# A two-block transformer layer on one core: the first block's steps in another order, and the memory's keys projected while experts are chosen

## The chip, the core and the metric

The kernel runs on one core of one Trainium2 chip. TensorE multiplies matrices and transposes, VectorE (DVE) and ScalarE (ACT) do the elementwise work, GpSimd (POOL) clears two tiles, and SyncE (SP) issues nearly all DMAs. Everything is in fp32. The metric is the device time of one execution in microseconds; lower is better.

## The reference

Two transformer blocks run one after the other on 256 tokens of width 1024. The first block has two mixers, a merge of both, and a layer of 64 experts. The second has three attention branches; the keys and values of one (cross attention) come from a second input, the memory, and from nothing that the first block computes.

```python
def first_block(x, ...):
        h = rmsnorm(x, attn_norm_w[l])
        z = h @ w_in[l]
        hq, hf, hi, hg, cq, ckv, kr, gate_a, gate_b = jnp.split(z, split_idx, axis=-1)
        o_a = hgrn2_mixer(hq, hf, hi, hg, lb_all[l], hg_out_norm_w[l]).astype(x.dtype)
        o_b = mla_mixer(cq, ckv, kr, positions, mla_q_norm_w[l], mla_w_uq[l], mla_kv_norm_w[l], mla_w_ukv[l])
        y = jax.nn.sigmoid(gate_a) * (o_a @ w_branch_hgrn[l]) + jax.nn.sigmoid(gate_b) * (o_b @ w_branch_mla[l])
        x = x + y @ w_out[l]
        h = rmsnorm(x, ffn_norm_w[l])
        x = x + hierarchical_moe(h, router_group_w[l], ...)   # top group, then its top 2 of 8 experts
    return rmsnorm(x, final_norm_w)

def hybrid_layer(x, mem, ...):
    h = rmsnorm_2(x, g_in)
    z = h @ w_in
    ...
    kv = rmsnorm_2(mem, g_mem) @ w_mem_kv
    xk = kv[..., :X_W].reshape(B, M, X_HEADS, X_HEAD_DIM)
    xv = kv[..., X_W:].reshape(B, M, X_HEADS, X_HEAD_DIM)
    yc = cross_attention(heads(xq, X_HEADS, X_HEAD_DIM), xk, xv).reshape(B, S, X_W)
    ...
    return x + u @ w_out
```

## The kernel before

**The plan.** `plan()` writes a list of steps, and every engine walks through the same list in the same order, taking from each step the part that is its own. So the list fixes the order on each engine, and semaphores tie the engines together. The steps that matter here:

- `proj` of a name is a projection of all 256 tokens by one unit of weights (mostly 1024 x 512): 32 matmul instructions of 256 columns (features in rows, L803) or 16 of 512 (tokens in rows). The hardware profiler records two passes for each fp32 matmul, so its counts are twice these; transposes are recorded once. Projections take turns on the PSUM tiles psP0 and psP1; all other steps use psA and psB.
- `hf`, `hq`, `hv`, `hg` belong to the first mixer (forget gate, queries, values, output gate). `level` 0 to 8 build its causal attention in nine steps: TensorE multiplies (L948), VectorE copies under a mask (L1511) and makes the operands of the next level by four products (L1298). A projection stands between any two levels.
- `cl` and `ch` give the latents of the second mixer, `cnorm` normalises them: squares and roots on ScalarE (L1214 to L1220), scaling on VectorE (L1537, L1538), 10 transposes on TensorE, a scaled copy on VectorE. `uq` projects queries from them, `kn` keys, `vm` values; `hg_out`, `hg_outT` finish the first mixer and transpose it; `qkpT` transposes the rotary parts.
- `scores` (TensorE, psA, L1029 and L1030), `soft` (VectorE scale and maximum, ScalarE exponentials), `normal` (VectorE division), `probsT` (TensorE transposes into psB, ScalarE copies out) and `pv` (TensorE into psB, VectorE copies out) do attention in three chunks, 0 to 2.
- `ga`, `gb` are gates; `wa` and `wb` project the mixers' outputs, `wo` the merged one, `rt` is the router. `norm mem` normalises the memory and transposes it (16 transposes). `rank` chooses the experts: a chain of small VectorE steps, five small matmuls (L1071 to L1075), again VectorE.
- `moe` is the expert loop. All weights of 64 experts go through four buffers of 4 MB, 96 chunks in all. TensorE first gathers tokens (32 passes, L467), then each chunk takes 32 or so passes (L481, L492). `xk`, `xv` project keys and values of the memory, at the start of the second block, while ScalarE and VectorE do its first norm (`stats`).

**Where weights lie.** Units go through `ring`, four slots of 2 MB. SyncE loads unit n when unit n-4 has been multiplied. The first four expert chunks are not allowed in before a projection each has finished (`before_chunk`: wb1, wo0, wo1, wo1), since they take the place of ring slots and of tiles in the `arena`. Chunk c from 4 on waits for `used`, a count that TensorE raises behind each chunk it has finished, to reach c-3.

**Where steps wait for each other.** The wait of a `proj` step on TensorE covers its weights, its PSUM tile (emptied by ScalarE or VectorE) and its inputs. wb0 waits for the last `pv`, wo0 for the evacuation of wb1. The MoE part of TensorE waits for `rt`, for the selection matrix and for the normalised tokens.

Of the kernel before, what the change touches and what calls it, by code (L numbers as in the profile page):

```python
# [29 lines left out]
S = 256  # L30
NT = S // P
D = 1024
KC = D // P
# [76 lines left out]
def units_2():  # L110
    kv = [("xk", "w_mem_kv_2", 0, 512, 8), ("xv", "w_mem_kv_2", 512, 512, 8)]
    u = [("iq", 4096), ("ikw", 4608), ("dq", 2048), ("dv", 3072), ("dk", 2560), ("mv", 1024), ("mq", 0),
         ("dg", 3584), ("mk", 512), ("mg", 1536)]
    u = kv + [(n, "w_in_2", c, 72 if n == "ikw" else 512, 8) for n, c in u]
    u += [("xq", "w_in_2", 4680, 512, 8), ("xg", "w_in_2", 5192, 512, 8)]
    u += [(f"gl{i}", "w_in_2", 5704 + 512 * i, 512, 8) for i in range(6)]
    u += [("um", "w_up_moba_2", 0, 1024, 4), ("ud", "w_up_dsa_2", 0, 1024, 4), ("ux", "w_up_cross_2", 0, 1024, 4)]
    u += [(f"w2{i}", "w_out_2", 512 * i, 512, 8) for i in range(2)]
    return u


UNITS_1, UNITS_2 = units_1(), units_2()


# [17 lines left out]
def plan():  # L142

    p = []
# [19 lines left out]
    proj("hf0", "hf1", "hq0", "hq1")  # L164
    p.append(("level", 0, "AB"))
    fill = [["hv0"], ["hv1"], ["cl"], ["ch"], ["hg0", "hg1"], ["ga0"], ["ga1"], ["gb0"]]
    for n in range(1, len(LEVELS) + 2):
        proj(*fill[n - 1])
        p.append(("level", n, "AB" if n <= len(LEVELS) else "A"))
    p.append(("cnorm", 0, "AB"))  # L170
    p.append(("hg_out", 0, "AB"))
    proj("gb1")
    proj("uq0n", "uq0p", "uq1n", "uq1p")
    p.append(("hg_outT", 0, "AB"))
    p.append(("qkpT", 0, "AB"))
    proj("kn0", "kn1")
    soft(0)
    proj("vm0", "vm1")
    turn(0, 1, "wa0")
    turn(1, 2, "wa1")  # L180
    p.append(("normal", 2, ""))
    p.append(("norm", "mem", "AB"))
    p.extend([("probsT", 2, "B"), ("pv", 2, "B")])
    proj("wb0", "wb1")
# [5 lines left out]
    proj("rt")  # L190
    p.append(("rank", 0, "A"))
    p.append(("moe", 0, ""))

    p.append(("stats", "mid", ""))
    proj("xk", "xv")
# [71 lines left out]
def build(nc, ins, out):  # L267
    with ExitStack() as ctx:
# [62 lines left out]
        memT = area(1, KC, S)  # L331
        mem = area(13, NT, D)
# [8 lines left out]
        xqT, xkT, xv = area(8, 4, S), area(8, 4, S, off=1024), area(9, NT, 512)  # L341
        ropeA, ropeB = area(9, NT, 512, off=1024), area(13, NT, 512)
        relu_s = area(13, 2, 512, off=1024)
# [5 lines left out]
        wrow, wrow_f = cT[:, 0:4, :].rearrange("p a b -> p (a b)"), area(13, D, off=1024)  # L349
# [36 lines left out]
        rt_in = sem("rt_in")  # L386
# [50 lines left out]
        def unit_ap(name):  # L437
            slot, _, _, (_, _, _, cols, kc) = unit_at[name]
            return ring[:, slot, 0:kc * cols].rearrange("p (k n) -> p k n", k=kc)

        def wait_unit(e, name):
            e.wait_ge(unit_at[name][1], unit_at[name][2])
# [16 lines left out]
        def moe_tensor(pe):  # L459
# [53 lines left out]
            pe.wait_ge(no_rows, 1)  # L513
            with pe.Fori(0, rounds) as r:
# [195 lines left out]
        def _(sp):  # L710
# [77 lines left out]
        def _(pe):  # L788
# [6 lines left out]

            def proj(key, name, lhs_of, rhs_of, kc, outs):

                may_fill(pe, key)
                r = region_of(key)
                for o in range(len(outs(ps[r]))):  # L800
                    dst = outs(ps[r])[o]
                    for k in range(kc):
                        mm = pe.matmul(dst, lhs_of(o, k), rhs_of(o, k), start=(k == 0), stop=(k == kc - 1))  # L803
                mm.then_inc(full[r], 1)
# [19 lines left out]
            for name, arg, _ in PLAN:  # L824
                key = (name, arg)
# [255 lines left out]
        def _(act):  # L1081
# [31 lines left out]
            for name, arg, _ in PLAN:  # L1113
                key = (name, arg)
                if name == "norm":
# [6 lines left out]
                    elif arg == "mem":  # L1122
                        act.wait_ge(mem_in, 16)
                        wait_full(act, ("scores", 2))
                        square_sums(lambda t: mem[:, t, :], lambda t: memT[:, :, :].rearrange("p k s -> p (k s)")[:, t * D:(t + 1) * D], 2, 16, D)
# [162 lines left out]
        def _(dve):  # L1288
# [68 lines left out]
            for name, arg, _ in PLAN:  # L1357
# [41 lines left out]
                elif name == "norm" and arg == "mem":  # L1399
# [3 lines left out]
                    i.then_inc(normed, 1)  # L1403
                    into_T(key, memT, V_MEM)
# [285 lines left out]
def laid_out(inputs):  # L1690

    given = {name: np.ascontiguousarray(inputs[name]) for name in _AS_THEY_ARE}
    for name, tensor, c0, cols, kc in UNITS_1 + UNITS_2:
# [47 lines left out]
```

## Time and profile before

| what | us |
|---|---|
| median of 3 runs | 1761.36 (1760.98 to 1761.41) |
| the profiled execution's own time | 1762.46 |
| its span, first to last instruction | 1760.6 |
| TensorE busy | 1384.9 |
| VectorE busy | 329.5 |
| ScalarE busy | 209.0 |
| mean granted TensorE clock | 0.893 of full speed |
| DMA | 504.43 MB, mean 287 GB/s |

The first block's mixers fill the first 430 us or so, the expert loop the next 920, the second block the last 410. The span is the figure to set a sum of the trace against; the run around it adds 1.9 us. In the tables below, idle time before an instruction stands in brackets with the engine that ended it.

### The profile page before, as it was taken

The numbers are of one execution on the slowest core, as the hardware profiler recorded it, in microseconds if no ns is written. First come the engines' busy times: TensorE is split into PE (matmuls) and PEld (weight loads), VectorE is DVE, ScalarE is ACT, GpSimd is POOL, SyncE is SP. The second block draws the span as 40 slices with busy tenths as digits, with TensorE's granted clock in tenths as the row PEclk, the third lists the DMA queues.
The fourth block names the chain that finished last, engine by engine and source line by source line (L and its number), as shares of the span: only waits on it lengthen the run. The fifth ranks groups of instructions, "written<-read, shape, count | busy, mean of one in ns | idle before, by whom it ended". The sixth has DMA issues, their size and how long they took to land.

```text
span 1760.6 us, 16409 instructions
## 1 busy us (share of the span) xinstructions
PE 1384.9 (79%) x7184; PEld 778.7 (44%) x7184; DVE 329.5 (19%) x585; ACT 209.0 (12%) x366; POOL 1.4 (0%) x6
## 2 busy tenths in 40 slices
PE   6999989888866676656666666666667999999996
PEld 5756886775322122212221222122214546788882
DVE  2233432312211001101010101010101221252221
ACT  1000032202000000000000000000001001143300
POOL 0000000000000000000000000000000000000000
PEclk9999998988987788878887888888878999999998
DMA  7324133317999999999999999999997433332310
GB/s 285 114 103 172 67 117 146 102 51 330 394 429 433 433 431 429 433 434 432 429 430 435 433 429 430 435 433 430 430 435 337 171 134 137 132 144 108 142 50 24
DMA packets 24550, 504.43 MB, mean 287 GB/s; under 512 B 4672, under 2 KB 4928, under 8 KB 6336
## 3 DMA queue, kind: packets, MB, share of 16 engines
q1 hardware_dynamic: 24080, 503.69, 68.6%
q8 instruction: 30, 0.49, 0.1%
q10 hardware_dynamic: 432, 0.17, 0.0%
q14 instruction: 8, 0.07, 0.0%
HBM read 502.81 MB, written 1.05 MB: 286 GB/s over the span
## 4 chain that ended last, share of the span: by engine, by line
PE 51%; DMA 44%; DVE 3%; ACT 1%; issue 1%; SPq 0%; DVEq 0%; ACTq 0%
DMA arena<-in_experts 44%; PE psP L803 35%; PE psP L481 5%; PE psP L492 3%; DVE arena L1298 2%; PE psB L1064 1%; PE psB L793 1%; PE psA L948 1%; PE psB L948 1%; PE psA L1030 1%; PE psA L1029 1%; PE psA L793 0%; PE psA L502 0%; PE psP L848 0%; PE psP L842 0%
## 5 line engine op out<-in xcount | busy, mean ns | idle before, releaser
L803 PE MATMUL psP<-arena,ring 128*128 128x256 f32 x1664 | 369.3, 384 | 2.2 <-DVE arena L1298 1.4
L803 PEld LDWEIGHTS psP<-arena,ring 128*128 128x128 f32 x1664 | 319.1, 193 | 48.1 <-issue 4.2
L481 PE MATMUL psP<-ring,arena 128*32 128x512 f32 x1024 | 162.1, 792 | 103.9 <-DMA ring<-in_experts 103.9
L803 PE MATMUL psP<-ring,arena 128*128 128x512 f32 (+2 forms) x576 | 233.1, 564 | 7.3 <-DVE arena L1298 7.3
L481 PE MATMUL psP<-arena 128*32 128x512 f32 x1024 | 158.1, 774 | 99.8 <-DMA arena<-in_experts 99.8
L1298 DVE TENSOR_TENSOR X<-X,psA 128x512 f32<-128x512 f32 x68 | 46.8, 688 | 682.1 <-PE psA L502 682.1
L803 PEld LDWEIGHTS psP<-ring,arena 128*128 128x128 f32 x576 | 105.7, 191 | 126.1 <-issue 126.0
L481 PEld LDWEIGHTS psP<-ring,arena 128*32 128x32 f32 x1024 | 41.0, 139 | 223.2 <-issue 176.5
L481 PEld LDWEIGHTS psP<-arena 128*32 128x32 f32 x1024 | 37.3, 136 | 217.9 <-DMA arena<-in_experts 126.5
L492 PE MATMUL psP<-arena 128*32 128x512 f32 x512 | 76.8, 754 | 53.6 <-DMA arena<-in_experts 49.8
L492 PE MATMUL psP<-ring,arena 128*32 128x512 f32 x512 | 73.4, 725 | 48.0 <-DMA ring<-in_experts 44.5
L467 PEld LDWEIGHTS psA<-arena 128*128 128x128 f32 x544 | 64.0, 197 | 15.1 <-issue 15.1
L502 PE MATMUL psA<-arena 128*128 128x512 f32 x136 | 67.4, 618 | 2.0 <-ACT arena L578 1.2
L467 PE MATMUL psA<-arena 128*128 128x128 f32 x544 | 67.2, 283 | 1.2 <-DVE small L627 1.2
L492 PEld LDWEIGHTS psP<-arena 128*32 128x32 f32 x512 | 18.1, 134 | 106.4 <-DMA arena<-in_experts 61.8
L1298 DVE TENSOR_TENSOR arena<-arena 128x1024 f32<-128x1024 f32 (+6 forms) x90 | 63.1, 729 | 1.2
L492 PEld LDWEIGHTS psP<-ring,arena 128*32 128x32 f32 x512 | 17.9, 129 | 97.9 <-issue 46.7
L1108 ACT ACTIVATE arena<-psP 128x1024 f32<-128x1024 f32 (+1 forms) x26 | 26.1, 1002 | 286.7 <-PE psP L803 286.7
L571 ACT ACT_TABLE_LOAD x16 | 20.5, 1283 | 276.6 <-PE psP L481 276.6
L573 ACT ACTIVATE arena<-psB 128x256 f32<-128x256 f32 x16 | 6.1, 383 | 333.3 <-PE psB L542 333.3
L578 ACT ACTIVATE arena<-psP 128x1024 f32<-128x1024 f32 x16 | 16.4, 1023 | 244.2 <-PE psP L492 244.2
L502 PEld LDWEIGHTS psA<-arena 128*128 128x128 f32 x136 | 23.0, 189 | 48.4 <-issue 44.6
(223 smaller groups left out, 748.3 us busy)
## 6 DMA issues: line engine op xcount, KB each, us to landing
arena<-in_experts SPq DMA_DIRECT2D x48, 4096.0 KB, 33.3
ring<-in_experts SPq DMA_DIRECT2D x48, 4096.0 KB, 33.3
ring<-in_u_gl SPq DMA_DIRECT2D x6, 2048.0 KB, 7.7
ring<-in_u_hf SPq DMA_DIRECT2D x2, 2048.0 KB, 11.9
ring<-in_u_hq SPq DMA_DIRECT2D x2, 2048.0 KB, 22.0
ring<-in_u_hv SPq DMA_DIRECT2D x2, 2048.0 KB, 7.7
ring<-in_u_hg SPq DMA_DIRECT2D x2, 2048.0 KB, 7.4
ring<-in_u_ga SPq DMA_DIRECT2D x2, 2048.0 KB, 7.5
```

Of the source, the lines that this page charges most:

```text
L467: mm = pe.matmul(zA[:, k * P:(k + 1) * P], xnf[:, t, k * P:(k + 1) * P], selA[:, t].rearrange("p j c -> p (j c)"), start=(t == 0), stop=(t ...
L481: mm = pe.matmul(z[j * CAP:(j + 1) * CAP, :], x[:, 4 * half + k, j * CAP:(j + 1) * CAP], held[c % 4][:, j, k * 512:(k + 1) * 512], start=( ...
L492: mm = pe.matmul(zY[j * CAP:(j + 1) * CAP, cols * 512:(cols + 1) * 512], hidT[:, 2 * half + f, j * CAP:(j + 1) * CAP], held[c % 4][:, j, f ...
L502: pe.matmul(zA[:, c:c + 512], selTs[:, t * P:(t + 1) * P], ysb[:, half * 512:(half + 1) * 512], start=True, stop=True).then_inc(scattered, 1)
L571: act.activation(gs, ps["P0"][:, 0:512], ACT.Silu).then_inc(gate_read, 1)
L793: mm = pe.transpose(ps[region][:, i * P:(i + 1) * P], src_of(i), ident)
L803: mm = pe.matmul(dst, lhs_of(o, k), rhs_of(o, k), start=(k == 0), stop=(k == kc - 1))
L948: mm = pe.matmul(ps[r][:, h * P:(h + 1) * P], k[:, h, t * P:(t + 1) * P], q[:, h, t * P:(t + 1) * P], start=True, stop=True)
L1029: pe.matmul(dst, qn[:, h, tt], kn[:, h, 0:nk], start=True, stop=False)
L1030: mm = pe.matmul(dst, qpeT[lo:lo + 64, h // 2, tt], kpeT[lo:lo + 64, 0:nk], start=False, stop=True)
L1108: act.activation(dst, view(ps[r]), func, **kw).then_inc(empty[r], 1)
L1298: return dve.tensor_tensor(o, a, b, op)
```

## The change

Five edits to the plan, and what they need:

1. `hv0` is projected ahead of level 0, and the other fillers between levels move up by one; `hg0` and `hg1` no longer stand together.
2. `cnorm` stands between level 5 and level 6, inside the projection `ga0`: 16 of its 32 matmuls, the latents' transposes, the other 16. A new step `head` runs a projection up to a given matmul and leaves it open in its PSUM tile. `gb1` now stands between level 8 and `hg_out`.
3. `kn0`, `kn1` stand ahead of `qkpT`, and `vm0` ahead of the first `scores`.
4. The last softmax: `scores` 2 and its softmax stay, but `probsT` 2 and `pv` 2 lie inside `wa1`, which is cut at 16 and 24 matmuls. The memory's statistics are a step `mnorm` behind `wa1`, and its 16 transposes stand behind `wb1`.
5. `xk` is projected around `rank`: 20 matmuls ahead of it, 12 behind. Its weights do not go through the ring any more. They have a place of their own (`wxk`, areas 10 and 11 of the arena), loaded behind the first expert chunk once `wb1` has been evacuated. `xkT`, `relu_s` and `wrow_f` change places in the arena. GpSimd waits for `xk` before it clears its tiles, which lie in area 11 and 13, and TensorE waits for the evacuation of `xk` before the loop.

```diff
 def units_2():
-    kv = [("xk", "w_mem_kv_2", 0, 512, 8), ("xv", "w_mem_kv_2", 512, 512, 8)]
+    kv = [("xv", "w_mem_kv_2", 512, 512, 8)]
...
-    proj("hf0", "hf1", "hq0", "hq1")
+    proj("hf0", "hf1", "hq0", "hq1", "hv0")
     p.append(("level", 0, "AB"))
-    fill = [["hv0"], ["hv1"], ["cl"], ["ch"], ["hg0", "hg1"], ["ga0"], ["ga1"], ["gb0"]]
+    fill = ["hv1", "cl", "ch", "hg0", "hg1", "ga0", "ga1", "gb0"]
     for n in range(1, len(LEVELS) + 2):
-        proj(*fill[n - 1])
+        if fill[n - 1] == "ga0":
+
+            p.append(("head", ("ga0", 16), ""))
+            p.append(("cnorm", 0, "AB"))
+        proj(fill[n - 1])
         p.append(("level", n, "AB" if n <= len(LEVELS) else "A"))
-    p.append(("cnorm", 0, "AB"))
+    proj("gb1")
     p.append(("hg_out", 0, "AB"))
-    proj("gb1")
     proj("uq0n", "uq0p", "uq1n", "uq1p")
     p.append(("hg_outT", 0, "AB"))
+    proj("kn0", "kn1")
     p.append(("qkpT", 0, "AB"))
-    proj("kn0", "kn1")
+    proj("vm0")
     soft(0)
-    proj("vm0", "vm1")
+    proj("vm1")
     turn(0, 1, "wa0")
-    turn(1, 2, "wa1")
+
+    p.append(("normal", 1, ""))
+    soft(2)
+    p.append(("probsT", 1, "B"))
+    p.append(("head", ("wa1", 16), ""))
+    p.append(("pv", 1, "B"))
     p.append(("normal", 2, ""))
+    p.append(("probsT", 2, "B"))
+    p.append(("head", ("wa1", 24), ""))
+    p.append(("pv", 2, "B"))
+    proj("wa1")
+    p.append(("mnorm", 0, ""))
+    proj("wb0", "wb1")
     p.append(("norm", "mem", "AB"))
-    p.extend([("probsT", 2, "B"), ("pv", 2, "B")])
-    proj("wb0", "wb1")
     proj("wo0")
...
     proj("rt")
+
+    p.append(("head", ("xk", 20), ""))
     p.append(("rank", 0, "A"))
+    proj("xk")
     p.append(("moe", 0, ""))
 
     p.append(("stats", "mid", ""))
-    proj("xk", "xv")
+    proj("xv")
...
+        wxk = area(10, KC, 512)
...
             pe.wait_ge(no_rows, 1)
+            wait_empty(pe, ("proj", "xk"))
...
                     sp.dma_start(held[c % 4].rearrange("p e n -> p (e n)"), src).then_inc(chunk_in[c % 4], 16)
+                    if peeled and c == 0:
+
+                        wait_empty(sp, ("proj", "wb1"))
+                        sp.dma_start(wxk, ins["u_xk"].rearrange("p (k n) -> p k n", k=KC)).then_inc(xk_in, 16)
...
             pool.wait_ge(rounds_ready, 1)
+            wait_full(pool, ("proj", "xk"))
             pool.memset(selTs, 0.0)
```

**The order on TensorE around the latents' norm.** Before, L948 and L954 are the levels, L803 projections (here `ga0`, `ga1`, `gb0`), L793 the latents' transposes and L973 `hg_out`:

```order
L948 MATMUL psA<-arena 128x128 x8
L948 MATMUL psB<-arena 128x128 x8
L803 MATMUL psP<-arena,ring 128x256 x32
L948 MATMUL psA<-arena 128x128 x8
L948 MATMUL psB<-arena 128x128 x8
L803 MATMUL psP<-arena,ring 128x256 x32
L954 MATMUL psA<-arena 128x128 x8
L793 MATMUL psA<-consts_sb,arena 128x128 x5
L793 MATMUL psB<-consts_sb,arena 128x128 x5
L973 MATMUL psA<-arena 128x128 x8
```

Of the change (L988, L994 the levels, L837 projections, L823 transposes):

```order
L988 MATMUL psA<-arena 128x128 x8
L988 MATMUL psB<-arena 128x128 x8
L837 MATMUL psP<-arena,ring 128x256 x16
L823 MATMUL psA<-consts_sb,arena 128x128 x5
L823 MATMUL psB<-consts_sb,arena 128x128 x5
L837 MATMUL psP<-arena,ring 128x256 x16
L988 MATMUL psA<-arena 128x128 x8
L988 MATMUL psB<-arena 128x128 x8
```

The ten transposes moved from behind the last level into the middle of `ga0`; behind the last level stands `gb1` now.

**The order on TensorE around the last softmax.** Before, L793 in psB alone is `probsT`, L1064 `pv`; x16 is the memory's second eight transposes with `probsT` 2 behind them, and the last row is `wb0`, `wb1`:

```order
L793 MATMUL psB<-consts_sb,arena 128x128 x8
L803 MATMUL psP<-arena,ring 128x256 x32
L1064 MATMUL psB<-arena 128x128 x8
L793 MATMUL psA<-consts_sb,arena 128x128 x8
L793 MATMUL psB<-consts_sb,arena 128x128 x16
L1064 MATMUL psB<-arena 128x128 x8
L803 MATMUL psP<-arena,ring 128x256 x64
```

Of the change:

```order
L823 MATMUL psB<-consts_sb,arena 128x128 x8
L837 MATMUL psP<-arena,ring 128x256 x16
L1104 MATMUL psB<-arena 128x128 x8
L823 MATMUL psB<-consts_sb,arena 128x128 x8
L837 MATMUL psP<-arena,ring 128x256 x8
L1104 MATMUL psB<-arena 128x128 x8
L837 MATMUL psP<-arena,ring 128x256 x72
L823 MATMUL psA<-consts_sb,arena 128x128 x8
L823 MATMUL psB<-consts_sb,arena 128x128 x8
```

`wa1` is in three pieces (16, 8, and 8 of the x72), with `pv` 1, `probsT` 2 and `pv` 2 between them, and the memory's transposes come behind all 64 matmuls of `wb`.

**The order on TensorE around the choice of experts.** Of the change; before, the rows of L837 are not there (L903 is the router's second half, L1111 to L1115 are `rank`, L491 the gather):

```order
L903 MATMUL psP<-rtw,arena 128x72 x8
L837 MATMUL psP<-arena 128x256 x20
L1111 MATMUL psA<-arena,consts_sb 128x64
L1112 MATMUL psA<-arena,consts_sb 128x64
L1113 MATMUL psA<-arena,consts_sb 128x64
L1114 MATMUL psA<-arena,consts_sb 128x64
L1115 MATMUL psA<-arena,consts_sb 128x64
L837 MATMUL psP<-arena 128x256 x12
L491 MATMUL psA<-arena 128x128 x16
```

All 32 matmuls of `xk` came in from the start of the second block.

## Rows read from the trace of the kernel before

**Rows 1.** The page: span, and the shares of the chain that ended last.

```profile
span 1760.6 us, 16409 instructions
...
PE 51%; DMA 44%; DVE 3%; ACT 1%; issue 1%; SPq 0%; DVEq 0%; ACTq 0%
```

**Rows 2.** Timeline of SP's issues (start, us, what): first expert chunk.

```profile
389.63 0.43 SPq L753 DMA_DIRECT2D arena<-in_experts  x1
```

**Rows 3.** Stretches: us, engines' busy time, PEclk, DMA share, GB/s.

```profile
402.00:406.00 4.00, 4.00 (x11) 1.84 (x10) 0.00 (x0) 0.00 (x0) 0.00 (x0) 1.00 0.04 16
...
441.00:444.00 3.00, 3.00 (x32) 0.74 (x24) 2.57 (x13) 0.00 (x0) 0.00 (x0) 1.00 0.28 120
...
460.00:1342.00 882.00, 576.72 (x3629) 195.99 (x3627) 85.28 (x138) 59.23 (x77) 0.00 (x0) 0.82 1.00 431
```

**Rows 4.** Timeline of PE: levels 0 and 4, latents' transposes, hg_out (brackets: idle before).

```profile
77.64 2.05 PE L948 MATMUL psA<-arena 128*128 128x128 f32 x16 [1.84 <-DVE arena L1433]
...
139.55 2.05 PE L948 MATMUL psA<-arena 128*128 128x128 f32 x16 [0.95 <-DVE arena L1298]
...
229.67 1.33 PE L793 MATMUL psA<-consts_sb,arena 128*128 128x128 f32 x5 [4.88 <-DVE arena L1538]
...
232.01 3.04 PE L973 MATMUL psA<-arena 128*128 128x128 f32 x16
```

**Rows 5.** Timeline of DVE: products behind level 4, latents' scaling begins, division of chunk 2.

```profile
144.62 4.86 DVE L1298 TENSOR_TENSOR arena<-arena 128x1024 f32<-128x1024 f32 x4
...
228.13 0.18 DVE L1305 RECIPROCAL small<-small 128x4 f32<-128x4 f32 x1 [2.07 <-ACT small L1218]
...
344.47 1.22 DVE L1298 TENSOR_TENSOR arena<-arena,small 128x1024 f32<-128x1024 f32 x1
```

**Rows 6.** Timeline of PE: rotary transposes, first scores, vm0 with vm1.

```profile
272.16 0.63 PE L984 MATMUL psA<-consts_sb,arena 128*128 128x128 f32 x4 [2.43 <-DVE arena L1563]
...
282.34 0.46 PE L1029 MATMUL psA<-arena 128*128 128x128 f32 x2 [1.41 <-issue]
...
291.65 9.07 PE L803 MATMUL psP<-ring,cT 128*128 128x512 f32 x16
```

**Rows 7.** Stretches, PE alone: us, busy (passes), PEclk, DMA share, GB/s; first scores.

```profile
282.00:285.00 3.00, 2.66 (x13) 1.00 0.00 0
285.00:288.00 3.00, 3.00 (x10) 0.56 0.00 0
```

**Rows 8.** Timeline of PE: pv 1, memory's transposes, pv 2, wb0 and wb1, wo0.

```profile
341.67 1.95 PE L1064 MATMUL psB<-arena 128*128 128x128 f32 x16
347.27 1.97 PE L793 MATMUL psA<-consts_sb,arena 128*128 128x128 f32 x8 [3.65 <-DVE arena L1402]
...
354.29 3.78 PE L1064 MATMUL psB<-arena 128*128 128x128 f32 x16 [1.17 <-ACT arena L1108]
358.90 30.31 PE L803 MATMUL psP<-arena,ring 128*128 128x256 f32 x128 [0.83 <-issue]
391.99 8.39 PE L803 MATMUL psP<-ring,arena 128*128 128x512 f32 x19 [2.78 <-DVE arena L1298]
```

**Rows 9.** Timeline of PE: rank, first gather, a gather in the loop.

```profile
431.17 0.69 PE L1071 MATMUL psA<-arena,consts_sb 128*128 128x64 f32 x2 [5.20 <-DVE arena L1298]
...
434.75 5.81 PE L467 MATMUL psA<-arena 128*128 128x128 f32 x32 [1.19 <-DVE small L627]
...
1327.86 3.84 PE L467 MATMUL psA<-arena 128*128 128x128 f32 x32
```

**Rows 10.** Timeline: last expert chunk, xk, second norm (DVE), xv.

```profile
1342.04 6.03 PE L492 MATMUL psP<-arena 128*32 128x512 f32 x32 [5.35 <-DMA arena<-in_experts]
...
1353.89 13.98 PE L803 MATMUL psP<-arena,ring 128*128 128x256 f32 x64
...
1364.24 1.42 DVE L1417 TENSOR_SCALAR arena<-X,small 128x1024 f32<-128x1024 f32 x2
1367.70 13.90 PE L803 MATMUL psP<-ring,arena 128*128 128x512 f32 x32
```

More of the change, by code:

```diff
@@ L122 @@
 UNITS_1, UNITS_2 = units_1(), units_2()
+UNIT_XK = ("xk", "w_mem_kv_2", 0, 512, 8)
 CAUSAL = [(0, 0, 8, 1), (1, 0, 4, 2), (1, 4, 4, 2)]
@@ L340, in build @@
         soft_2, prT_2 = area(6, 2, 1024), area(7, 2, 8, P)
-        xqT, xkT, xv = area(8, 4, S), area(8, 4, S, off=1024), area(9, NT, 512)
+        xqT, xkT, xv = area(8, 4, S), area(13, 4, S, off=1024), area(9, NT, 512)
         ropeA, ropeB = area(9, NT, 512, off=1024), area(13, NT, 512)
-        relu_s = area(13, 2, 512, off=1024)
+        relu_s = area(8, 2, 512, off=1024)
         score = sb("score", [P, 384])
@@ L348, in build @@
         gl = [area(0, KC, S), area(1, KC, S), area(2, KC, S)]
-        wrow, wrow_f = cT[:, 0:4, :].rearrange("p a b -> p (a b)"), area(13, D, off=1024)
+        wrow, wrow_f = cT[:, 0:4, :].rearrange("p a b -> p (a b)"), area(8, D, off=1024)
         ps = {"P0": ctx.enter_context(nc.psum_tensor("psP0", [P, 1024], F32)),
@@ L385, in build @@
         used = sem("used")
-        rt_in = sem("rt_in")
+        rt_in, xk_in = sem("rt_in"), sem("xk_in")
         rt_scaled, wo_half, ffn_sums, tokens_ready = sem("rt_scaled"), sem("wo_half"), sem("ffn_sums"), sem("tokens_ready")
@@ L437, in unit_ap @@
         def unit_ap(name):
+            if name == "xk":
+                return wxk
             slot, _, _, (_, _, _, cols, kc) = unit_at[name]
@@ L441, in wait_unit @@
         def wait_unit(e, name):
+            if name == "xk":
+                e.wait_ge(xk_in, 16)
+                return
             e.wait_ge(unit_at[name][1], unit_at[name][2])
@@ L794, in transposes @@
                 mm.then_inc(full[region], 1)
+            begun = {}
             def proj(key, name, lhs_of, rhs_of, kc, outs):
-                may_fill(pe, key)
                 r = region_of(key)
[L800 to L804, printed above, removed]
+                dsts = outs(ps[r])
+                if name not in begun:
+                    may_fill(pe, key)
+                stop_at = upto or len(dsts) * kc
+                for i in range(begun.get(name, 0), stop_at):
+                    o, k = i // kc, i % kc
+                    mm = pe.matmul(dsts[o], lhs_of(o, k), rhs_of(o, k), start=(k == 0), stop=(k == kc - 1))
+                begun[name] = stop_at
+                if stop_at == len(dsts) * kc:
+                    mm.then_inc(full[r], 1)
             def rows_out(cols):
@@ L824, in _ @@
             for name, arg, _ in PLAN:
+                upto = None
+                if name == "head":
+                    name, (arg, upto) = "proj", arg
                 key = (name, arg)
@@ L1121, in _ @@
                         act.activation(vec[:, V_LB:V_LB + 8], vec[:, V_LB:V_LB + 8], ACT.Sigmoid).then_inc(lb_sig, 1)
[L1122 to L1125, printed above, removed]
+                elif name == "mnorm":
+                    act.wait_ge(mem_in, 16)
+                    wait_full(act, ("scores", 2))
+                    square_sums(lambda t: mem[:, t, :], lambda t: memT[:, :, :].rearrange("p k s -> p (k s)")[:, t * D:(t + 1) * D], 2, 16, D)
                 elif name == "xT":
@@ L1398, in _ @@
                     link(dve.tensor_scalar(vec[:, V_OML:V_OML + 8], vec[:, V_LB:V_LB + 8], -1.0, 1.0, ALU.mult, ALU.add))
-                elif name == "norm" and arg == "mem":
+                elif name == "mnorm":
                     inverse_root(18)
@@ L1403, in _ @@
                     i.then_inc(normed, 1)
+                elif name == "norm" and arg == "mem":
                     into_T(key, memT, V_MEM)
@@ L1692, in laid_out @@
     given = {name: np.ascontiguousarray(inputs[name]) for name in _AS_THEY_ARE}
-    for name, tensor, c0, cols, kc in UNITS_1 + UNITS_2:
+    for name, tensor, c0, cols, kc in UNITS_1 + UNITS_2 + [UNIT_XK]:
         if tensor != "router":
```

## The prediction

> **What bounds the kernel now.** I read the chain that ended last first. It is half TensorE and 44% DMA [rows 1], so there are two kinds of stretch, and the table of stretches shows where each lies. From 460 to 1342 us the DMA engines are full at 431 GB/s, and TensorE waits for expert chunks [rows 3]. That stretch has a fixed length for its bytes: 92 chunks are issued from the first `used` on, at 444 us (the gather ends at 434.75 + 5.81 = 440.6, its first chunk takes some 3.6 us), and the last one is met at 1342.0 [rows 9, 10], so 898 us / 92 = 9.76 us for each. Nothing that TensorE does inside the loop changes it. What changes the time is when the first `used` comes, and what follows the last chunk. Both are TensorE's chain. Next I read TensorE's timeline for idle time in brackets, and the granted clock beside it, because each wait costs twice: the wait, and slower matmuls behind it. After the 4.88 us of idle at 224.8, 16 passes of `hg_out` took 3.04 us, where the same 16 take 1.95 to 2.05 in the levels [rows 4].
>
> At the loop's start the four buffers are loaded early and DMA stands nearly still from 441 to 444 (120 GB/s) [rows 3], so the start hangs on TensorE reaching its first chunk, not on data.
>
> **Unit prices.** A projection is 13.8 us at full clock (1353.89 to 1367.70) [rows 10]: 0.432 for each of 32 matmuls. An attention product `pv` is 1.8 (16 passes, 1.95 with the overlap), eight transposes some 0.9.
>
> **The latents' norm and level 0.** Gone: the 1.84 us before level 0, since `hv0` now covers ScalarE and VectorE there; the 4.88 us of idle before the transposes; their 2.34 us (229.67 to 232.01); and about 1.1 us of slow `hg_out`. Sum 10.2 [rows 4]. Added in the middle of `ga0`: the ten transposes at full clock, 1.1 us, and a wait. VectorE is queued with level 5's work first: from a level's first matmul to the end of its four products it takes 139.55 to 149.48 = 9.9 us, then the scaling takes 228.13 to 229.67 = 1.5 [rows 4, 5], so the scaled latents come 11.4 us behind level 5's start. ScalarE's part is hidden in this, as it starts once `hg1` has been copied out. TensorE has 3.7 us of level and 16 x 0.432 = 6.9, together 10.6. It waits 0.9 us; if the scaling were late for another reason, at most the old 4.9. I take 0.9: the row of level 4 with 0.95 is the nearest. Behind the waiting transposes stand the other 16 matmuls of `ga0` and level 6, whose operands are ready by then. Net **-8.2** (bounds -10.2 + 1.1 and -4.2). The 0.95 us wait behind the short `ch` stays; it moves one level up.
>
> **First scores.** `kn0` and `kn1`, 6.9 us, cover VectorE's 2.43 us, and `vm0`, 3.5 us, covers the copies out behind the rotary transposes, the 1.41 us [rows 6]. Both covers are longer than the waits, so **-3.8**. The softmax of chunk 0 took 291.65 to 299.2 before and has to hide in `vm1` (3.5) and `scores` 1 (4.9), 8.4 us against 7.5; it hides narrowly. The clock is the unsure part. It fell during the first scores: 1.00 until 285, 0.56 after [rows 7]. The 16 score matmuls took 282.34 to 291.65 = 9.3 us. The 13 passes by 285 make about 0.415 us for each matmul, 6.65 in all at full clock, so 2.7 us were lost there; and `vm0` with `vm1` took 9.07 where 16 x 0.432 = 6.9, so 2.1 more. Of these 4.8 us the change gives back between nothing (the scores are as thin as before, and they alone last 6.7 us) and all (there is no idle ahead of them now). Neither end has a nearer row; I take the middle, **-2.4**.
>
> **Last softmax.** Before, from the start of `wa1` at 327.9 (341.67 less 13.8) to the end of `wb1` at 358.90 + 30.31 = 389.2 are 61.3 us [rows 8]. After, the same stretch is `wa1` 13.8, `pv` 1 1.8, a wait, `probsT` 2 0.9, `pv` 2 1.8, and `wb` 27.6, without the memory's transposes. The wait: VectorE took from the end of `pv` 1 at 343.5 through its copy out and the division to 344.47 + 1.22 = 345.7 [rows 5], so 2.2 us; nothing is put under it. `pv` 1 itself waits for ScalarE's copy of the transposed probabilities, which in the timeline came 5.9 us after `probsT` 1 began, against 0.9 + 6.9 of cover: no wait. `pv` 2 needs 1.1 us after `probsT` 2, under 8 matmuls of 3.5. Sum 48.1 + 0.1: **-13.1**. Bounds: if the 2.2 us of waiting brought the clock down as the 3.65 did (transposes at 1.97 for eight, `pv` 2 at 3.78, 2.7 us more in `wb`) [rows 8], some 5 us less; if it hid wholly, 2 more.
>
> The memory's transposes, 1.8 us, go under the 2.78 us that `wo0` waits anyway for the evacuation of `wb1` [rows 8]: nothing. Without that cover they would cost 1.8.
>
> **The keys around the choice.** Added 13.8 us of matmuls. Taken away: the idle 5.20 and 1.19 that TensorE spent waiting for VectorE's choice; the slow clock behind it: `rank` took 431.17 to 433.56 = 2.4, its ten passes at full clock about 1.2, and the gather 5.81 against 3.84 in the loop [rows 9]. So 13.8 - 6.4 - 1.2 - 2.0 = **+4.2** to the first `used`. Twenty matmuls, 8.6 us, are more than the 5.2 that VectorE needs, so `rank` starts 3.4 late and VectorE waits for it. GpSimd's two memsets wait for `xk` too, but take 1.3 us against the gather's 3.8. Bounds: +7.4 if the clock fell all the same. Below +4.2 there is little to find, since TensorE is then busy without a break from the router to the first chunk.
>
> SyncE is moved past one more DMA: behind chunk 0 it waits for `wb1`'s evacuation, 2.6 us, and issues 2 MB. Behind it is queued chunk 1, which waits for the end of `wo0` anyway. The 2 MB take 4.9 us at 431 GB/s, and DMA stood still at 16 GB/s from 402 to 406 [rows 3], between chunk 0 (issued at 389.63) [rows 2] and chunk 1. Nothing; 4.9 us if it is not so.
>
> **Second block.** `xv` follows the loop directly. Its norm is ready at 1364.24 + 1.42 = 1365.7, 11.8 us behind the loop's end, and `xv` alone is 13.8: hidden, with 2 us to spare [rows 10]. The ring's loads come one unit earlier, never later. **-13.8**. If the norm or a load were late, 2 us less.
>
> **The sum.** -8.2 - 3.8 - 2.4 - 13.1 + 4.2 - 13.8 = -37.1. Against the profiled execution (1762.46 us, span 1760.6) that is 1725.4; it lies 1.1 over the median of 1761.36, so for a median **1724.3 us**.
>
> **A rule weighed.** In the trace the clock fell at 285 while TensorE was busy with scores and its last idle time was 1.41 us [rows 6, 7]. The Trainium skill (TensorE: Matmul & The Clock Gate, section "HAM oscillation — how this bites in real kernels") has the rule that re-throttling comes from idle gaps, and that keeping the engine fed keeps it warm. By that rule the new first scores, with no gap ahead, stay at the full 2.4 GHz; by the row they are thin work and may fall again to 1.2 GHz.
>
> **Rivals.**
> - *The clock stays up through the first scores.* For it: no idle ahead. Against it: it fell 3 us into the same matmuls, and they go on for 6.7 now. It gives the other 2.4 us: 1721.9.
> - *The waits of the split projections bring the clock down*, at the cut in `ga0` or behind `pv` 1, where the wait of 2.2 us has thin transposes beside it. Against it: 2.78 us of idle before `wo0` did no harm [rows 8], its 8.39 us for 19 passes being full speed. Some 5 to 7 us: 1731.
> - *The keys' weights get in the stream's way*, chunk 1 to 3 being pushed back until the first `used` is no longer what starts the stream: 2 MB more ahead of it, 4.9 us: 1729.
> - *Slower than before: the stream itself.* The loop has 92 chunks at 9.76 us. If the moved weights or the shifted start made it 0.41 us longer for each chunk (a rate under 413 GB/s instead of 431), the whole gain would be gone; at 0.5 us the time is 1770. Nothing in the rows points to it: the bytes in the loop are the same.
> - *The change does not do what it says*: `rank`, held up 3.4 us, and the norms end later than TensorE. All edits are on TensorE's own order, which the listings show, so only the sizes can be wrong.
>
> **How the numbers follow.** Forecast 0.52 (1724, between 1720 and 1728); clock up 0.22; clock brought down by waits 0.14; keys in the way 0.06; stream slower 0.03; the rest 0.03. The tail adds noise of its own: the last chunk's matmuls took 6.03 us where others with the same count take 3.6, by the clock of the moment. Range **1717 to 1731**: the clock case less 2.4 us of that noise and 2 for waits hidden better, and up to the case of the waits. Faster by over 0.2% (3.5 us, about what a measurement of this kernel tells from no change) 0.96, same 0.01, slower 0.03.
>
> **What would show it.** After: no idle over 1 us before the latents' transposes, with level 6 starting at about 188 as before; first scores at about 273; `wb1` ending 28 us earlier than 389.2, near 361; first expert chunk multiplied 23 us earlier, at about 417.5; the last chunk met near 1319; `xv` directly behind the loop. Wrong would be: a first chunk started earlier without the last one being met as much earlier (then the stream, not its start, is the bound), idle time before `rank` or the gather, or a second-block norm that ends after `xv`.

## Result, and the profile after

| | before | after |
|---|---|---|
| median, us | 1761.17 (1760.85 to 1761.41, 4 runs) | 1721.29 (1720.90 to 1721.53, 4 runs) |
| span of the profiled execution | 1760.6 | 1719.7 |
| TensorE busy | 1384.9 | 1364.5 |
| mean granted clock | 0.893 | 0.904 |

The ratio is 0.9775, 95% interval 0.9763 to 0.9787: 39.9 us faster. The forecast was 1724.3, 3.0 above the result. It lies inside the forecast's own 1720 to 1728, but nearest to the rival in which the clock stays up through the first scores (1721.9), and the rows below show that this is what happened.

The page of after, its PEclk and GB/s rows in 40 slices and the chain that ended last:

```profile
span 1719.7 us, 16411 instructions
...
PEclk9999999999888788888887888888878999999998
...
GB/s 292 116 131 130 88 146 123 105 256 316 429 428 436 428 434 431 429 434 430 434 431 430 434 430 434 431 429 434 431 434 380 147 146 147 139 107 118 140 49 24
...
PE 51%; DMA 45%; DVE 3%; ACT 1%; issue 0%; SPq 0%; DVEq 0%; ACTq 0%
```

The two kinds of stretch are still there (half TensorE, 45% DMA); both ends of TensorE's part became shorter.

The timeline of PE, after: level 4, the latents' transposes in the middle of `ga0`, level 6, the first scores, `vm1`, `probsT` 2, `wb` and `wo0` (start, us, what; in brackets the idle time before). It answers to [rows 4, 6, 8].

```profile
133.88 2.05 PE L988 MATMUL psA<-arena 128*128 128x128 f32 x16 [0.95 <-DVE arena L1338]
...
179.88 0.77 PE L823 MATMUL psA<-consts_sb,arena 128*128 128x128 f32 x5 [0.64 <-DVE arena L1579]
...
187.94 1.95 PE L988 MATMUL psA<-arena 128*128 128x128 f32 x16
...
272.40 0.39 PE L1069 MATMUL psA<-arena 128*128 128x128 f32 x2
...
278.96 3.70 PE L837 MATMUL psP<-ring,cT 128*128 128x512 f32 x8
...
320.78 1.09 PE L823 MATMUL psB<-consts_sb,arena 128*128 128x128 f32 x8 [2.13 <-DVE arena L1338]
...
326.95 31.25 PE L837 MATMUL psP<-arena,ring 128*128 128x256 f32 x144
360.98 13.97 PE L837 MATMUL psP<-ring,arena 128*128 128x512 f32 x32 [1.03 <-DVE arena L1338]
```

The 4.88, 2.43 and 1.41 us of idle are gone, and 0.64 came in their place; so are the 1.84 us before level 0 and 0.36 us between the rotary transposes. Around the last softmax 2.13 us stand for 3.65, 1.41, 1.17 and 0.83, and `wo0` waits 1.03 instead of 2.78. The 16 score matmuls last from 272.40 to 278.96 = 6.6 us, against 9.3.

The same timeline around the choice of experts, and at the loop's end [rows 9, 10]:

```profile
394.80 8.85 PE L837 MATMUL psP<-arena 128*128 128x256 f32 x40
...
403.48 0.33 PE L1111 MATMUL psA<-arena,consts_sb 128*128 128x64 f32 x2
...
404.54 5.40 PE L837 MATMUL psP<-arena 128*128 128x256 f32 x24
409.77 3.73 PE L491 MATMUL psA<-arena 128*128 128x128 f32 x32
413.44 3.64 PE L505 MATMUL psP<-arena 128*32 128x512 f32 x32
...
1315.00 5.86 PE L516 MATMUL psP<-arena 128*32 128x512 f32 x32 [5.35 <-DMA arena<-in_experts]
...
1326.68 13.90 PE L837 MATMUL psP<-ring,arena 128*128 128x512 f32 x32
1340.42 1.04 PE L823 MATMUL psA<-consts_sb,arena 128*128 128x128 f32 x8
```

`rank` takes 1.06 us instead of 2.4, and nothing stands between it, the rest of `xk`, the gather and the first chunk. The first chunk is multiplied 27.06 us earlier (440.50 before), the last one 27.04 earlier: the stream is 901.5 us long in both. `xv` stands directly behind the loop, and the norm's transposes directly behind `xv`.

Stretches of after (us, busy time and passes of PE, PEld, DVE, ACT, POOL, then PEclk, DMA share, GB/s): the first scores, `probsT` 2, the choice of experts, and the loop.

```profile
270.00:280.00 10.00, 10.00 (x41) 6.17 (x41) 0.93 (x1) 2.96 (x4) 0.00 (x0) 1.00 0.01 2
...
320.00:324.00 4.00, 3.22 (x19) 2.97 (x20) 0.72 (x1) 2.03 (x4) 0.00 (x0) 1.00 0.00 0
...
400.00:413.00 13.00, 13.00 (x80) 11.96 (x79) 2.49 (x12) 1.79 (x6) 1.20 (x2) 1.00 0.85 365
...
460.00:1310.00 850.00, 555.17 (x3502) 189.01 (x3494) 81.95 (x133) 57.22 (x74) 0.00 (x0) 0.82 1.00 432
```

TensorE's clock is at its upper level, 2.4 GHz, in the first three; before, it was at 0.56 in the first scores [rows 7]. The page's first ten slices show 9 throughout.

### The profile page after: what moved, and what is told of

It is laid out like the page before. It is cut to its first block, busy times and chain, and to the rows that moved or that the text cites. A ratio compares the mean times of both kernels' runs of the same rounds, so it can differ in the third digit from the quotient of the medians.

```text
span 1719.7 us, 16411 instructions
## 1 busy us (share of the span) xinstructions
PE 1364.5 (79%) x7184; PEld 767.4 (45%) x7184; DVE 329.4 (19%) x585; ACT 207.5 (12%) x365; POOL 1.4 (0%) x6
## 4 chain that ended last, share of the span: by engine, by line
PE 51%; DMA 45%; DVE 3%; ACT 1%; issue 0%; SPq 0%; DVEq 0%; ACTq 0%
DMA arena<-in_experts 45%; PE psP L837 35%; PE psP L505 5%; PE psP L516 3%; DVE arena L1338 2%; PE psB L1104 1%; PE psB L823 1%; PE psA L988 1%; PE psB L988 1%; PE psA L1070 0%; PE psA L526 0%; PE psA L1069 0%; PE psP L888 0%; PE psP L882 0%; PE psA L823 0%
## 5 line engine op out<-in xcount | busy, mean ns | idle before, releaser
L837 PE MATMUL psP<-arena,ring 128*128 128x256 f32 x1600 | 353.0, 383 | 1.4 <-DVE arena L1338 1.4
L837 PEld LDWEIGHTS psP<-arena,ring 128*128 128x128 f32 x1600 | 305.8, 192 | 43.3 <-issue 2.6
L837 PE MATMUL psP<-ring,arena 128*128 128x512 f32 (+2 forms) x576 | 233.2, 564 | 5.6 <-DVE arena L1338 5.6
L837 PEld LDWEIGHTS psP<-ring,arena 128*128 128x128 f32 x576 | 106.0, 192 | 124.0 <-issue 123.8
L505 PEld LDWEIGHTS psP<-arena 128*32 128x32 f32 x1024 | 37.1, 136 | 217.5 <-DMA arena<-in_experts 127.0
L491 PEld LDWEIGHTS psA<-arena 128*128 128x128 f32 x544 | 62.1, 192 | 13.7 <-issue 13.6
L491 PE MATMUL psA<-arena 128*128 128x128 f32 x544 | 65.2, 279 | 0.0
```

Of the source, the lines that this page charges most:

```text
L491: mm = pe.matmul(zA[:, k * P:(k + 1) * P], xnf[:, t, k * P:(k + 1) * P], selA[:, t].rearrange("p j c -> p (j c)"), start=(t == 0), stop=(t ...
L505: mm = pe.matmul(z[j * CAP:(j + 1) * CAP, :], x[:, 4 * half + k, j * CAP:(j + 1) * CAP], held[c % 4][:, j, k * 512:(k + 1) * 512], start=( ...
L837: mm = pe.matmul(dsts[o], lhs_of(o, k), rhs_of(o, k), start=(k == 0), stop=(k == kc - 1))
```

## Experiments

**How they are compared.** Each kernel undoes or changes one part of the changed kernel. Spans alone mislead by up to 2.7 us. TensorE's first transposes, at 13 us, take 1.94 us for eight, where eight take 1.04 later, so the clock starts at its lower level; in some executions it has come up before the first projection starts at 18 us, in others some microseconds later. The granted clock of the stretch reads 1.00 either way; the passes show it. The first line is of after, the second of the kernel with its remaining waits covered (section "The waits that are left"), both from 16 to 23 us (us, PE busy and passes, PEclk, DMA share, GB/s):

```profile
16.00:23.00 7.00, 5.59 (x17) 1.00 1.03 441
```

```profile
16.00:23.00 7.00, 5.59 (x27) 1.00 1.04 442
```

17 passes against 27 in the same busy time; a pass takes 0.216 us at full clock (13.8 us for 64), and 27 of them are about 5.6. So beside the median I give the time from the end of the first four projections (75.8 us in before and after, 73.1 to 75.6 in the others) to the first expert chunk: 364.70 in before, 337.64 in after.

### Each edit undone

The first two edits together, the latents' norm behind the last level and `hv0` behind level 0 again:

```diff
-    proj("hf0", "hf1", "hq0", "hq1", "hv0")
+    proj("hf0", "hf1", "hq0", "hq1")
...
-            p.append(("head", ("ga0", 16), ""))
-            p.append(("cnorm", 0, "AB"))
...
-    proj("gb1")
+    p.append(("cnorm", 0, "AB"))
     p.append(("hg_out", 0, "AB"))
+    proj("gb1")
```

> The changed kernel with the first two edits undone: hv0 behind level 0, the latents' norm behind the last level, hg_out ahead of gb1. My sum has 8.2 us for these, so 1729.5 if the other parts keep their gain. Rival, that waits are simply made up for later by other slack: 1721 to 1724. If the clock is what the waits cost most, the 4.9 us of idle behind the last level should be followed by passes at half speed again.

Measured: 1730.88 us (1728.84 to 1731.25), ratio to before 0.9827 (0.9811 to 0.9843); 347.47 us to the first chunk, 9.8 more than after. Its timeline of PE, at the latents' transposes and at the last softmax:

```profile
229.36 0.94 PE L820 MATMUL psA<-consts_sb,arena 128*128 128x128 f32 x5 [4.88 <-DVE arena L1576]
...
328.57 1.80 PE L820 MATMUL psB<-consts_sb,arena 128*128 128x128 f32 x8 [2.13 <-DVE arena L1335]
330.16 4.63 PE L834 MATMUL psP<-arena,ring 128*128 128x256 f32 x16
```

The 4.88 us are back. But 1.7 of the 9.8 us do not lie in this edit's stretch: behind the 2.13 us wait of the last softmax, which both kernels have, 16 passes take 4.63 us here and 3.62 in after, and the transposes 1.80 against 1.09. Up to `uq0` the kernel is 8.1 us behind after, beside the 8.2 of the sum.

`kn0`, `kn1` behind `qkpT` and `vm0` behind the first scores again:

```diff
-    proj("kn0", "kn1")
     p.append(("qkpT", 0, "AB"))
-    proj("vm0")
+    proj("kn0", "kn1")
     soft(0)
-    proj("vm1")
+    proj("vm0", "vm1")
```

> The changed kernel with kn0, kn1 and vm0 back in their old places around the rotary transposes and the first scores. Waits of 3.8 to 4.2 us come back. Theory of idle time: the clock falls again in the first scores, with 4.8 us more, so 1730. Theory of thin work, where something else kept the clock up in the changed kernel (where the scores lie in time): only the waits come back, 1725.5.

Measured: 1731.19 us (1729.36 to 1735.73), ratio 0.9834 (0.9814 to 0.9855); 350.45 to the first chunk, 12.8 more than after. The stretches of this kernel, waits and `kn`, then the scores:

```profile
260.00:276.00 16.00, 12.87 (x56) 10.40 (x56) 2.44 (x2) 5.08 (x7) 0.00 (x0) 0.89 0.26 106
276.00:286.00 10.00, 10.00 (x24) 5.89 (x23) 2.62 (x3) 0.66 (x3) 0.00 (x0) 0.51 0.01 2
```

and its timeline, the three waits:

```profile
261.39 0.63 PE L1023 MATMUL psA<-consts_sb,arena 128*128 128x128 f32 x4 [2.44 <-DVE arena L1603]
262.49 1.04 PE L1023 MATMUL psB<-consts_sb,arena 128*128 128x128 f32 x4 [0.36 <-DVE arena L1603]
263.55 8.30 PE L836 MATMUL psP<-cT,ring 128*128 128x256 f32 x32
...
273.23 0.46 PE L1068 MATMUL psA<-arena 128*128 128x128 f32 x2 [1.38 <-issue]
...
282.51 9.10 PE L836 MATMUL psP<-ring,cT 128*128 128x512 f32 x16
```

The clock fell again during the same matmuls (0.51 from 276 us on, 2.8 us into them), and once before, from the second rotary transposes into `kn`: the waits cost 4.2 us, the slow clock some 6.8 (the projection behind the first waits took 8.30 us against 7.07 in after, the transposes, the scores and `vm` the rest), and another 1.7 came behind the last softmax's wait (its transposes 1.09 us here, the 16 passes behind them 5.31). So this edit is worth the most, and more than half of it is clock. The four executions of this kernel lie 6.4 us apart; the longest has the lowest mean clock (0.898, against 0.903 in the two shortest), so how much the clock costs here isn't the same each time.

The last softmax behind `wa1`, the memory's norm under it again:

```diff
-    p.append(("normal", 1, ""))
-    soft(2)
-    p.append(("probsT", 1, "B"))
-    p.append(("head", ("wa1", 16), ""))
-    p.append(("pv", 1, "B"))
+    turn(1, 2, "wa1")
     p.append(("normal", 2, ""))
...
-    proj("wb0", "wb1")
     p.append(("norm", "mem", "AB"))
+    p.extend([("probsT", 2, "B"), ("pv", 2, "B")])
+    proj("wb0", "wb1")
```

> The changed kernel with the last softmax and the memory's norm as before (wa1 whole, probsT 2 and pv 2 behind the memory's transposes, which stand ahead of wb0). My sum has 13.1 us for this part, so 1734.4; without the half clock behind the waits it would be some 8.6 of them, 1730.

Measured: 1729.45 us (1728.85 to 1730.63), ratio 0.9824 (0.9808 to 0.9841); 347.94 to the first chunk, 10.3 more than after. In the timeline of PE the waits of before are all there, but the clock fell for less time:

```profile
326.78 1.97 PE L816 MATMUL psA<-consts_sb,arena 128*128 128x128 f32 x8 [3.66 <-DVE arena L1435]
...
331.71 1.06 PE L816 MATMUL psB<-consts_sb,arena 128*128 128x128 f32 x8 [1.41 <-DVE arena L1331]
333.95 3.42 PE L1097 MATMUL psB<-arena 128*128 128x128 f32 x16 [1.17 <-ACT arena L1141]
338.20 27.86 PE L830 MATMUL psP<-arena,ring 128*128 128x256 f32 x128 [0.83 <-issue]
```

`wb` took 27.86 us, 30.31 before [rows 8]. That difference of 2.45 us is nearly all of the gap between 10.3 us and the 12.9 that this stretch gave in the change itself. The time agrees with the second of the two expectations, 1730, and not with the 1734.4 of the sum.

The keys at the start of the second block, through the ring:

```diff
-    kv = [("xv", "w_mem_kv_2", 512, 512, 8)]
+    kv = [("xk", "w_mem_kv_2", 0, 512, 8), ("xv", "w_mem_kv_2", 512, 512, 8)]
...
-    p.append(("head", ("xk", 20), ""))
     p.append(("rank", 0, "A"))
-    proj("xk")
...
-    proj("xv")
+    proj("xk", "xv")
```

> The changed kernel with xk back at the start of the second block, its weights through the ring. Theory: 13.8 us come back behind the loop and 4.2 go from the front of it, so 9.6 us more, 1730.9, with TensorE idle 5.2 us ahead of rank and its clock down through the gather. Rival, that the front part is not what starts the stream: 13.8 more, 1735.1.

Measured: 1730.53 us (1729.13 to 1731.44), ratio 0.983 (0.9814 to 0.9846). The first chunk comes 4.0 us sooner than in after (333.60 against 337.64), and from it to the end there are 1320.1 us against 1306.3: 13.9 more. Both terms of the sum, +4.2 and -13.8, are confirmed. The timeline of PE:

```profile
397.91 0.69 PE L1098 MATMUL psA<-arena,consts_sb 128*128 128x64 f32 x2 [5.19 <-DVE arena L1325]
...
401.50 5.72 PE L484 MATMUL psA<-arena 128*128 128x128 f32 x32 [1.20 <-DVE small L644]
```

The waits of 5.2 and 1.2 us and the gather of 5.7 us are those of before [rows 9]: nothing else in the change had touched them.

### Idle time or thin work

What brought the clock down in the first scores? The changed kernel with the scores of chunk 0 twice:

```diff
-                    for i, hl in enumerate(slots(kind, nh)):
+                    for i, hl in list(enumerate(slots(kind, nh))) * (2 if arg == 0 else 1):
```

> The changed kernel with each of the 16 score matmuls of chunk 0 issued twice (same operands and place, so the output is unchanged). They took 6.6 us at full clock in the changed kernel, with no idle time ahead of them. If the clock fell in the kernel before because of the idle time ahead of the scores, it stays up here too and the kernel is 6.6 us longer, about 1728. If thin work alone brings it down once it goes on long enough, the 13.2 us of it are enough (it fell 3 us into them before), and the scores and the projection behind them cost 3 to 10 us more, 1731 to 1738.

Measured: 1726.78 us (1725.28 to 1727.78), beside 1720.52 for the changed kernel on the same chip: 6.3 more; 344.30 to the first chunk, 6.7 more. The stretch with all 32 score matmuls:

```profile
272.00:286.00 14.00, 14.00 (x67) 9.82 (x66) 0.69 (x1) 2.31 (x2) 0.00 (x0) 1.00 0.00 1
```

Twice the thin work, 13.2 us on end, at the full 2.4 GHz. With the waits ahead of it the clock fell some 3 us into half as much. So thin work alone does not do it. Nor is it needed: in the second block of the changed kernel a projection of 512 columns stands behind a wait of 2.78 us, with a projection ahead of the wait too.

```profile
1677.87 29.40 PE L837 MATMUL psP<-ring,arena 128*128 128x512 f32 x64 [2.78 <-DVE arena L1338]
```

It takes 29.40 us, where the same 64 passes take 27.70 in one execution of the kernel with the four waits covered (below), and the granted clock is 0.50 from 1678 to 1681 us. So it was the idle time. By the rule of the Trainium skill (TensorE: Matmul & The Clock Gate, section "HAM oscillation — how this bites in real kernels"), which puts re-throttling down to idle gaps, this was to be expected, and the trace agrees: without a gap there was no fall. Not every gap brings one, though: the 2.13 us behind `pv` 1 in the changed kernel did not.

### What the keys' matmuls cost where they stand

The changed kernel with `xk` summed over the first 128 of 1024 features only, all of it behind `rank` (28 of 32 matmuls are left out):

```diff
-    p.append(("head", ("xk", 20), ""))
     p.append(("rank", 0, "A"))
     proj("xk")
...
-                        feature_major(key, arg, memT)
+                        feature_major(key, arg, memT, kc=1)
```

> The changed kernel with the memory's keys projected from the first 128 of 1024 features only, in one piece behind the ranking: 28 of 32 matmuls, 12.1 us, are left out, with them a part of the computation. If the keys lie fully on the path, the time falls by 12.1 us to about 1709. If, as the sum has it, most of them stand in for idle time and slow clock around the choice of the experts, the waits of 5.2 and 1.2 us and the half clock come back, and only 2 to 5 us are gained: 1717 to 1719.

Measured: 1716.15 us (1712.27 to 1720.15), 4.4 less than the changed kernel; 333.08 to the first chunk, 4.6 less. The executions lie 7.9 us apart, for a reason that is not known, and touch those of the changed kernel, so the 4.6 is the figure to go by. Timeline of PE:

```profile
399.70 0.69 PE L1110 MATMUL psA<-arena,consts_sb 128*128 128x64 f32 x2 [5.20 <-DVE arena L1337]
...
401.89 3.04 PE L836 MATMUL psP<-arena 128*128 128x256 f32 x8
404.77 3.73 PE L490 MATMUL psA<-arena 128*128 128x128 f32 x32
```

Leaving out 12.1 us of matmuls bought 4.6 us. The rest went back into the 5.20 us wait and into half clock behind it: `rank` took 2.2 us against 1.06 in after, and eight passes 3.04, where `xk` in after does 24 in 5.40. The wait of 1.2 us before the gather did not come back, as those eight passes stand in it.

### The waits that are left

The changed kernel with its four waits of the first block covered:

```diff
-            p.append(("head", ("ga0", 16), ""))
+            p.append(("head", ("ga0", 18), ""))
...
+        if fill[n - 1] == "ch":
+            p.append(("head", ("hg0", 2), ""))
...
-    p.append(("pv", 1, "B"))
     p.append(("normal", 2, ""))
+    p.append(("pv", 1, "B"))
+    p.append(("head", ("wa1", 19), ""))
     p.append(("probsT", 2, "B"))
-    p.append(("head", ("wa1", 24), ""))
+    p.append(("head", ("wa1", 26), ""))
...
+    p.append(("head", ("wo0", 4), ""))
     proj("wo0")
...
-                        wait_empty(pe, ("proj", "wb1"))
+                        if upto is None:
+                            wait_empty(pe, ("proj", "wb1"))
```

> The changed kernel with the four waits that are left in the first block covered: two matmuls of hg0 ahead of the level that waits 0.95 us, the cut of ga0 two matmuls later (0.64), the normal work and more of wa1 around the last softmax (2.13), four matmuls of wo0 ahead of wb1's evacuation (1.03). If each wait is on the path by its own length: 4.7 us less, 1716.6. If the waits only move to the next operand that is late, 0 to 2 us less.

Measured: **1712.99 us** (1710.62 to 1714.87), ratio to before 0.9731 (0.9717 to 0.9744), against 1720.52 for the changed kernel in the same comparison. It is the fastest version here. In its timeline of PE no bracket is left between the first four projections and `rt`; around the last softmax it reads:

```profile
313.72 1.46 PE L841 MATMUL psP<-arena,ring 128*128 128x256 f32 x6
315.01 1.04 PE L827 MATMUL psB<-consts_sb,arena 128*128 128x128 f32 x8
315.89 3.19 PE L841 MATMUL psP<-arena,ring 128*128 128x256 f32 x14
...
384.56 2.00 PE L907 MATMUL psP<-rtw,arena 128*128 128x72 f32 x16 [0.78 <-DVE arena L1709]
```

To the first chunk it is 5.7 us shorter, for 0.95 + 0.64 + 2.13 + 1.03 = 4.75 us of waits: each cost about 0.2 us more than its bracket. Groups without a wait between them overlap by some 0.17 us in the timeline (in after, 13.90 us of projection start at 1326.68 and the next group at 1340.42), and a wait ends that overlap. The other 1.8 us of the difference of medians lie outside the edited stretch. They fit the start and the second block, where this profile has no half clock behind the waits of the last softmax and the changed kernel's has (15.66 and 29.40 us for the two rows that take 13.98 and 27.70 below), but the executions at the medians of the two kernels were not both profiled, so this is not shown. The expectation, 1716.6, was 3.6 us too high: 1.0 us is what the waits cost beyond their brackets, 1.8 this, and the rest its start from 1721.3 instead of 1720.5.

The changed kernel itself, on that chip:

> The changed kernel once more, on the chip of the other three: 1721 within 2 us, as the time at which the clock comes up at the start moves every execution by up to 2.4 us.

Measured: 1720.52 us (1719.07 to 1721.20), ratio 0.9768 (0.9755 to 0.9782); 337.63 to the first chunk, as the 337.64 of after.

### Is the fall of the clock chance?

The same wait was followed by half clock in some kernels and not in others. Three kernels were profiled once more, unchanged.

> The kernel with the latents' norm and level 0 put back, once more. In its first profile the 2.13 us wait of the last softmax was followed by 3.4 us at half clock, where the same wait did nothing in the changed kernel. If that is fixed by the program's timing, it comes again at about 328 us; if it hangs on when the clock comes up at the start (which moved by up to 6 us and makes the first four projections end at 73 or 75.5 us), it comes again only if that is the same.

Measured: 1730.42 us; 347.43 to the first chunk (347.47). Timeline of PE, the same place:

```profile
328.09 1.77 PE L820 MATMUL psB<-consts_sb,arena 128*128 128x128 f32 x8 [2.13 <-DVE arena L1335]
```

> The kernel with the last softmax put back, once more. Its first profile had 6.8 us at half clock around the memory's transposes and pv 2, the kernel before 13.6 us at the same waits (3.65, 1.4, 1.17, 0.83 us). If the amount is fixed by the program's timing behind the start: 6.8 us again and 347.9 us from the end of the first four projections to the first expert chunk. If it is chance: up to 3.4 us of time more.

Measured: 1728.60 us; 347.88 (347.94). Again 27.86 us for `wb`:

```profile
333.70 3.40 PE L1097 MATMUL psB<-arena 128*128 128x128 f32 x16 [1.17 <-ACT arena L1141]
337.94 27.86 PE L830 MATMUL psP<-arena,ring 128*128 128x256 f32 x128 [0.83 <-issue]
```

> The kernel with the four waits covered, once more: 331.9 us from the end of the first four projections to the first expert chunk, as those waits and no half clock are in it; the rest moves with the start, by up to 2.4 us.

Measured: 1714.62 us; 331.92 (331.94). Here the start was the late one, the first at 73.1, this one at 75.6. The second block's last softmax, in the first profile and in the second:

```profile
1621.54 1.09 PE L827 MATMUL psB<-consts_sb,arena 128*128 128x128 f32 x8 [2.13 <-DVE arena L1343]
1622.47 13.98 PE L841 MATMUL psP<-arena,ring 128*128 128x256 f32 x64
...
1668.67 27.70 PE L841 MATMUL psP<-ring,arena 128*128 128x512 f32 x64 [2.81 <-DVE arena L1343]
```

```profile
1622.45 1.49 PE L827 MATMUL psB<-consts_sb,arena 128*128 128x128 f32 x8 [2.12 <-DVE arena L1343]
1623.74 15.30 PE L841 MATMUL psP<-arena,ring 128*128 128x256 f32 x64
...
1671.24 29.18 PE L841 MATMUL psP<-ring,arena 128*128 128x512 f32 x64 [2.78 <-DVE arena L1343]
```

To the first chunk, all three repeat within 0.1 us, half clock included. So it is not mere chance. Whether the order of work alone fixes it is not shown: the two kernels that have half clock in this stretch started alike both times (their first four projections end at 75.5 and 75.0 us, and at 73.4 and 73.2). The third started differently, and there the same two waits of 2.1 and 2.8 us in the second block cost some 3 us of slow clock in one execution and nothing in the other. (From the first chunk to the end the two differ by only 1.5 us, as the stream and its last matmuls were 1.6 us shorter in the second.) What exactly decides was not settled.

## Why the prediction was right, point by point

The stretches, before to after, by the points where both kernels start the same work:

| term | forecast | measured | from |
|---|---|---|---|
| latents' norm and level 0 | -8.2 | -8.6 | `uq0` at 252.28 and 243.67 |
| first scores, waits and clock | -3.8 - 2.4 | -9.5 | `wa0` at 306.41 and 288.34 |
| last softmax | -13.1 | -12.9 | `wo0` at 391.99 and 360.98 |
| keys around the choice | +4.2 | +4.0 | first chunk at 440.50 and 413.44 |
| second block | -13.8 | -13.8 | first chunk to the end, 1320.1 and 1306.3 |
| sum | -37.1 | -40.9 | spans 1760.6 and 1719.7 |

- **What bounds the kernel** was right. The stream kept its 901.5 us from first to last chunk, so what TensorE saved ahead of it came off the end in full. The keys' weights (issued at 360.75, chunk 1 at 374.98) pushed nothing back.
- **The latents' norm.** The wait of 0.9 us before the transposes was 0.64. The sum of VectorE's queue, level 5's products first and the scaling behind them, was the right way to place the latents.
- **The first scores: the mis-sized term.** The clock was taken at the middle of nothing and 4.8 us, -2.4, with the argument that it had fallen inside thin work which stays thin. All of it came back (the scores 2.75 us shorter, `vm` 1.9). The fall 3 us into the scores was read as a mark against the rival, when it was the late effect of the 2.43, 0.36 and 1.41 us of idle ahead; the doubled scores show that the thin work alone does nothing. So the case that came was a rival's, given 0.22; the forecast's own, with half of the slow clock left, did not come, and its number was near because the term was small. The wait of 0.36 us was left out of the -3.8 besides. The last half microsecond of the 3.3 us of error is spread over this stretch: the groups around the three waits take about 0.2 us less for each wait that is gone, as found with the four remaining waits.
- **The last softmax.** The new wait behind `pv` 1 was put at 2.2 and was 2.13, and the covers under `pv` 1, under `pv` 2 and under the memory's transposes held. Undone alone, this edit is worth only 10.3 us: most of the other 2.6 were slow clock that a kernel with slightly other timing does not pay. That forecast and measurement agree so closely has some luck in it.
- **The keys.** The trade was sized within 0.2 us: 13.8 us of matmuls for 6.4 of idle and 3.2 of slow clock. `rank` being held up harmed nobody.
- **The rivals.** The waits of the split projections did not bring the clock down in the changed kernel, but the one of 2.13 us did in two kernels that differ from it only earlier, for 1.7 us and not for 5 to 7. The trace of before had this price, and the prediction missed it: in its second block a wait of 2.13 us at the last softmax and one of 2.78 us before the last projection were each followed by slow clock (the projections from 1671.01 and 1718.86 us took 15.66 and 29.40 us for 64 passes, where the kernel with the four waits covered takes 13.98 and 27.70), 1.7 us each. The 2.78 us before `wo0`, which did no harm, were only one side of that evidence. A stream made slower by each chunk, or held up by the keys' weights, was not seen.

## What to carry to other kernels

Where the trace shows a lower granted clock behind waits, as here, price a wait twice: its own length, and the slower work behind it, which may begin some microseconds later and inside an innocent piece of work. Look for the same wait everywhere in the trace, since it may be followed by slow clock in one place and not in another. Put any independent matmuls into waits, even the front part of a projection whose later half needs an operand that is not ready: four waits of together 4.75 us gave 5.7 when covered, and 12.1 us of matmuls around a choice cost 4.6. When comparing variants whose difference is a few microseconds, line them up at a point behind the start: start and slow clock moved the two profiled executions of one kernel by 4.0 us, and repeats of others lay up to 7.9 us apart.

## What was not expected of the hardware

- The start: the same 7 us from 16 us on hold 17 or 27 passes of TensorE, though the granted clock of both stretches reads 1.00. The first four projections end at 73.1 to 73.6 us or at 75.0 to 75.8, and that difference is still there at the first expert chunk.
- A wait of 2.13 us behind `pv` 1 was followed by half clock in two kernels (the 16 passes behind the transposes took 4.63 and 5.31 us) and not in others (3.62); the two of these kernels that were run again, one of each kind, did the same. In one kernel two waits of 2.1 and 2.8 us in the second block did so in one execution and not in another.
- Doubled thin work, 13.2 us of matmuls of 128 columns, kept the clock at 2.4 GHz.
